# Rotary partners by four SP transfers from one whole ScalarE copy, in a two-layer attention kernel on one core

## What is computed

```python
def rope(x, pos):
    dh = x.shape[-1]
    freqs = ROPE_THETA ** (-jnp.arange(0, dh, 2, dtype=jnp.float32) / dh)
    ang = pos.astype(jnp.float32)[:, None] * freqs[None, :]
    cos = jnp.cos(ang)[None, :, None, :].astype(x.dtype)
    sin = jnp.sin(ang)[None, :, None, :].astype(x.dtype)
    x1, x2 = x[..., : dh // 2], x[..., dh // 2:]
    return jnp.concatenate([x1 * cos - x2 * sin, x2 * cos + x1 * sin], axis=-1)
...
q = rope(qkv[:, :, 0], pos)
k = rope(qkv[:, :, 1], pos)
```

## Time and profile before

| | us |
|---|---|
| median of three runs | 2187.29 |
| lowest and highest | 2184.91, 2189.29 |
| the profiled execution's own time | 2186.33 |
| its span, from first to last instruction | 2184.5 |
| busy: TensorE | 2103.2 (96%) |
| busy: VectorE | 955.9 (44%) |
| busy: ScalarE | 866.1 (40%) |
| busy: GpSimd | 837.4 (38%) |

### The profile page before, as it was taken

How to read it: one execution, slowest core, us unless ns; L and a number is a source line. 1 busy time by engine, 2 the same in 40 slices (tenths; PEclk the granted TensorE clock), 3 DMA queues, 4 the chain that set the end, 5 groups by cost and what they waited for, 6 DMA issues and landing times. The chain is left out here.

```text
span 2184.5 us, 26673 instructions
## 1 busy us (share of the span) xinstructions
PE 2103.2 (96%) x10336; PEld 1680.2 (77%) x10336; DVE 955.9 (44%) x1642; ACT 866.1 (40%) x1769; POOL 837.4 (38%) x447
## 2 busy tenths in 40 slices
PE   8999999999989989999999999999999899999998
PEld 6788898887768767778778788787774478888886
DVE  2454635544454585653442511268667532111212
ACT  4654556555364565542321332333332232221221
POOL 4423233333342332354444444334243152444443
PEclk9999999999999999999999999999999999999999
DMA  6322233223541312132443333332344242323331
GB/s 222 97 59 89 67 97 98 78 82 94 197 164 43 95 49 68 58 116 92 121 135 97 97 79 112 86 92 87 111 145 135 89 143 68 97 97 97 97 97 58
DMA packets 130204, 218.67 MB, mean 100 GB/s; under 512 B 8712, under 2 KB 58552, under 8 KB 129872
## 3 DMA queue, kind: packets, MB, share of 16 engines
q1 hardware_dynamic: 111152, 169.68, 26.0%
q0 software_dynamic: 8096, 28.93, 4.0%
q10 hardware_dynamic: 10832, 18.35, 2.4%
HBM read 198.29 MB, written 18.04 MB: 99 GB/s over the span
## 5 line engine op out<-in xcount | busy, mean ns | idle before, releaser
L2536 POOL TENSOR_TENSOR lo_ring<-raw_ring,hi_ring 128x1024 fp32r<-128x1024 f32 (+1 forms) x288 | 692.1, 2425 | 1002.2 <-ACT hi_ring L2179 1002.0
L1123 PE MATMUL bank<-xh,hi_ring 128*128 128x512 f32 (+1 forms) x1568 | 610.9, 390 | 3.5 <-DVE xl L1607 2.9
L1123 PE MATMUL bank<-xh,lo_ring 128*128 128x512 f32 (+1 forms) x1568 | 594.1, 379 | 0.0
L1123 PE MATMUL bank<-xl,hi_ring 128*128 128x512 f32 (+1 forms) x1568 | 592.8, 378 | 0.0
L2179 ACT CAST hi_ring<-raw_ring 128x1024 fp32r<-128x1024 f32 (+1 forms) x288 | 288.3, 1045 | 422.9 <-PE bank L1123 400.0
L1123 PEld LDWEIGHTS bank<-xh,hi_ring 128*128 128x128 f32 x1568 | 297.1, 190 | 66.3 <-issue 13.8
L1123 PEld LDWEIGHTS bank<-xh,lo_ring 128*128 128x128 f32 x1568 | 296.6, 189 | 56.2
L1123 PEld LDWEIGHTS bank<-xl,hi_ring 128*128 128x128 f32 x1568 | 297.4, 190 | 52.4 <-issue 1.9
L1123 PE MATMUL bank<-hi_ring,xh 128*128 128x512 f32 (+1 forms) x512 | 209.6, 409 | 8.2 <-DVE xl L1761 2.9
L1123 PE MATMUL bank<-hi_ring,xl 128*128 128x512 f32 (+1 forms) x512 | 201.4, 393 | 0.0
L1123 PE MATMUL bank<-lo_ring,xh 128*128 128x512 f32 (+1 forms) x512 | 201.3, 393 | 0.0
(11 more groups left out here) (289 smaller groups left out, 2650.1 us busy)
## 6 DMA issues: line engine op xcount, KB each, us to landing
raw_ring<-in_ffn_w_in SPq DMA_DIRECT2D x176, 256.0 KB, 3.2
raw_ring<-in_dil_w_in SPq DMA_DIRECT2D x80, 512.0 KB, 3.7
raw_ring<-in_ffn_w_out SPq DMA_DIRECT2D x44, 512.0 KB, 4.0
raw_ring<-in_diff_w_in SPq DMA_DIRECT2D x32, 512.0 KB, 3.8
raw_ring<-in_w_in SPq DMA_DIRECT2D x32, 512.0 KB, 3.7
arena<-scratch_heads POOLq DMA_DIRECT2D x4, 1584.0 KB, 13.8
scratch_gates<-arena ACTq DMA_DIRECT2D x24, 256.0 KB, 2.0
arena<-scratch_gates POOLq DMA_DIRECT2D x24, 256.0 KB, 5.2
```

Source lines behind the costliest of these rows:

```text
L1123: ins = T.matmul(bank[pb][:, cols if p.form == "feature" else slice(0, p.cols)], lhsT, rhs, start=(k == 0 and m == 0 and half != 1), stop= ...
L2536: G.tensor_tensor(lo, raw_ring[:, p % RAW, 0:q.kq * q.n], hi.bitcast(F32), ALU.subtract).then_inc(lowered, 1)
```

## The change

- ScalarE copies the whole bank once, 128 x 512, into `rope_b`. It waits first until `rope_rest` of the bank two before is done, since that reads the same half of `rope_b`.
- SP shifts: for each rotary bank four transfers of 32 partitions x 512 (64 KB), from `rope_b` to the partner's place in `QT` or `KT`, where the result will later stand. They signal `shifted`, one semaphore for even and one for odd banks.
- `rope_rest` waits for `shifted` in place of `drained`, takes the partner from `QT` or `KT` and writes the sin product into `rope_b`. It comes two banks later, not one, so that the cos products need a third place, the last 512 columns of `arena`.
- `rope_end` finishes the last two banks. It stands at the head of attention (directly before the first `d_score` or `f_score`) for units 0 to 3, 6 and 7, and behind the second `mac` of the `vt` panel for units 4 and 5.
- SP's program walks through the jobs. It loads up to 4 pieces beyond those that ScalarE splits at that job; in a rotary step it does so at bank 3, and in a panel's last step that is behind the shifts of banks 0 to 2. A shift waits for `drained`.
- Pool's load of the row `post0`, which lies in the third place, waits for all 48 banks of the dilated layer.

```diff
@@ rope_end: at the end of keys and projections before, now in attention
-        plan.job("rope_end")
...
+            if m == 1:
+                plan.job("rope_end", u)
...
         g = u // 2
+        if g < 2:
+            plan.job("rope_end", u)
@@ SP
+            def shift(p, o):
+                m = 4 * p.n + o
+                SP.wait_ge(drained[o], p.use[o])
+                for quad in range(4):
+                    SP.dma_start(rope_to(p, o)[32 * quad:32 * quad + 32], rope_b[32 * (quad ^ 1):32 * (quad ^ 1) + 32, m % 2, :]).then_inc(shifted[m % 2], 16)
...
+                elif kind == "mac":
+                    st = steps[a[0]]
+                    p = panels[st.panel]
+                    if place(*a) == st.look_at:
+                        wanted = st.ahead + RAW
+                    if p.kind != "rope" or a[1] == 3:
+                        load(wanted)
+                    if p.kind == "rope" and st.last and a[2:] != (0,):
+                        shift(p, a[1])
@@ VectorE
-            def rope_rest(which, u, o, m):
-                dst, b = (QT if which == "q" else KT)[:, u % 2, o, :], m % 2
-                V.wait_ge(drained[o], pending_use[m])
-                V.tensor_tensor(rope_b[:, b, :], rope_b[:, b, :], const("sin"), ALU.mult).then_inc(v_step, own.up())
+            def rope_rest(p, o):
+                m, dst = 4 * p.n + o, rope_to(p, o)
+                V.wait_ge(shifted[m % 2], 64 * (m // 2 + 1))
+                V.tensor_tensor(rope_b[:, m % 2, :], dst, const("sin"), ALU.mult).then_inc(v_step, own.up())
...
-                    if m >= 2:
-                        V.wait_ge(roped, m - 1)
-                    V.tensor_tensor(rope_a[:, o % 2, :], psum, const("cos"), ALU.mult).then_inc(cosed, 1)
-                    while pending:
-                        rope_rest(*pending.pop())
-                    pending.append((which, u, o, m))
+                    if m >= 3:
+                        V.wait_ge(roped, m - 2)
+                    V.tensor_tensor(cos_part[m % 3], psum, const("cos"), ALU.mult).then_inc(cosed, 1)
+                    if len(pending) == 2:
+                        rope_rest(*pending.pop(0))
+                    pending.append((p, o))
@@ ScalarE
                     A.wait_ge(cosed, m + 1)
-                    for quad in range(4):
-                        ins = A.copy(rope_b[32 * quad:32 * quad + 32, o % 2, :], psum[32 * (quad ^ 1):32 * (quad ^ 1) + 32, :])
-                    ins.then_inc(drained[o], 1)
+                    if m >= 2:
+                        A.wait_ge(roped, m - 1)
+                    A.copy(rope_b[:, m % 2, :], psum).then_inc(drained[o], 1)
```

More of the change, by code:

```diff
@@ L513, in keys @@
     def keys(u):
-        yield from plan.panel("rope", w, D + u * 512, 512, "feature", at=("k", 6 + u))
-        plan.job("rope_end")
+        return plan.panel("rope", w, D + u * 512, 512, "feature", at=("k", 6 + u))
     def attention(u):
@@ L521, in attention @@
         yield
+        plan.job("rope_end", 6 + u)
         for n in range(N + 4):
@@ L1004, in program @@
         y_panel = {p.w: p for p in panels if p.kind == "y" and p.at[0] == 1}
-        roped, cosed = sem("roped"), sem("cosed")
+        roped, cosed, shifted = sem("roped"), sem("cosed"), [sem(f"shifted{i}") for i in range(2)]
+        cos_part = [rope_a[:, 0, :], rope_a[:, 1, :], arena[:, ARENA - S:ARENA]]
         gate_tanhed, e_tanhed, hidden_rounded, hidden_made = sem("gate_tanhed"), sem("e_tanhed"), sem("hidden_rounded"), sem("hidden_made")
@@ L1057, in ready_value, with rope_to, load @@
             return made[name_value[0]], name_value[1]
+        def rope_to(p, o):
+            return (QT if p.at[0] == "q" else KT)[:, p.at[1] % 2, o, :]
         def sync_program(SP):
[L1060 to L1063, removed]
+            seen = Tally()
+            def load(limit):
+                while seen.n < min(limit, len(pieces)):
+                    p = seen.n
+                    seen.up()
+                    q = pieces[p]
+                    if p >= RAW:
+                        old = pieces[p - RAW]
+                        if old.parted:
+                            SP.wait_ge(lowered, old.split + 1)
+                        else:
+                            SP.wait_ge(*ready_value(steps[old.step].end))
+                    dst = raw_ring[:, p % RAW, 0:q.kq * q.n].rearrange("p (k n) -> p k n", k=q.kq)
+                    w = q.n // q.halves
+                    for i in range(q.halves):
+                        c = q.c0 + i * FFN
+                        src = I[q.w][q.k0 * P:(q.k0 + q.kq) * P, c:c + w].rearrange("(k p) n -> p k n", p=P)
+                        SP.dma_start(dst[:, :, i * w:(i + 1) * w], src).then_inc(landed[p % RAW], 16)
+            def shift(p, o):
[3 more added lines that the diff above has]
+                    SP.dma_start(rope_to(p, o)[32 * quad:32 * quad + 32], rope_b[32 * (quad ^ 1):32 * (quad ^ 1) + 32, m % 2, :]).then_inc(shifted[m % 2], 16)
+            wanted = RAW
+            for job in jobs:
+                kind, a = job.kind, job.at
+                if kind == "begin":
+                    SP.dma_start(consts[:, 0:P], I["consts"][:, 0:P]).then_inc(ident_landed, 16)
+                    SP.dma_start(x[:, 1, :], I["x"][P:2 * P, :]).then_inc(x_landed[1], 16)
+                    load(1)
@@ L1064, in sync_program @@
                     SP.dma_start(x[:, 3, :], I["x"][3 * P:4 * P, :]).then_inc(x_landed[3], 16)
-                if p == RAW:
+                    load(RAW)
                     SP.dma_start(consts[:, P:], I["consts"][:, P:]).then_inc(consts_landed, 16)
                     SP.dma_start(params[:, :], I["params"]).then_inc(consts_landed, 16)
[L1068 to L1079, removed]
+                elif kind == "lower_to":
+                    wanted = a[0] + RAW
+                    load(wanted)
+                elif kind == "mem_kv":
+                    wanted = steps[a[0]].ahead + RAW
+                    load(wanted)
+                elif kind == "mac":
[4 more added lines that the diff above has]
+                    if p.kind != "rope" or a[1] == 3:
+                        load(wanted)
+                    if p.kind == "rope" and st.last and a[2:] != (0,):
+                        shift(p, a[1])
@@ L1081, in tensor_program @@
+            load(len(pieces))
         def tensor_program(T):
@@ L1513, in vector_program @@
             pending = []
[L1515 to L1520 removed]
+            def rope_rest(p, o):
+                m, dst = 4 * p.n + o, rope_to(p, o)
+                V.wait_ge(shifted[m % 2], 64 * (m // 2 + 1))
+                V.tensor_tensor(rope_b[:, m % 2, :], dst, const("sin"), ALU.mult).then_inc(v_step, own.up())
+                r = DIL[p.at[1] // 2] if p.at[1] < 6 else 1
+                o_, a, c = dst, cos_part[m % 3], rope_b[:, m % 2, :]
                 if r > 1:
@@ L1526, in rope_rest @@
                 V.tensor_tensor(o_, a, c, ALU.add).then_inc(roped, 1)
-            pending_use = {}
             def consume(p, o):
@@ L1537, in consume @@
                 elif p.kind == "rope":
-                    which, u = p.at
                     V.wait_ge(filled[o], p.use[o])
-                    if which == "q" and u == 5 and o < 2:
-                        V.wait_ge(filled[6], use_of["v_turn", 2 + o][0])
-                    pending_use[m] = p.use[o]
-                    if m >= 2:
-                        V.wait_ge(roped, m - 1)
-                    V.tensor_tensor(rope_a[:, o % 2, :], psum, const("cos"), ALU.mult).then_inc(cosed, 1)
-                    while pending:
-                        rope_rest(*pending.pop())
-                    pending.append((which, u, o, m))
+                    if p.at == ("q", 5) and o == 0:
+                        V.wait_ge(filled[6], use_of["v_turn", 3][0])
+                    if m >= 3:
[4 more added lines that the diff above has]
+                    pending.append((p, o))
                 elif p.kind == "hid" and o < 2:
@@ L2029, in vector_program @@
                 elif kind == "rope_end":
-                    rope_rest(*pending.pop())
+                    while pending and pending[0][0].at == ("k", a[0]):
+                        rope_rest(*pending.pop(0))
                 elif kind == "norm_scale":
@@ L2582, in gpsimd_program @@
                 elif kind == "row":
+                    if a[0] == "post0":
+                        G.wait_ge(roped, 48)
                     if a[0] == "post1":
```

## The result

The changed kernel takes 2231.69 us, the median of four runs (2226.38 to 2233.66). Its ratio to the kernel before is 1.021, with a 95% interval of 1.020 to 1.023: slower by 2.1%, some 46 us over the 2186.1 us of the kernel before beside it, against the 13 us of the forecast. The profiled execution took 2233.66 us, its span 2231.9.

The account below looks back on a forecast made before the run. PE, busy 96% of the span, was taken to bound the kernel. Stalls of 14.4 plus clock loss of 7.1 less a gain of 8.2 gave +13.3 us on 2186.3: 2199.6 us, 0.6% slower, range 2191 to 2207.

Parts of the forecast that it names:

- the sin or add before them drawn out to the end of a Pool subtraction: Sign that the forecast is right: VectorE's sin or add before PE's `d_score` waits at units 0 to 3 lasts that long.
- part 2: SP and the transfers: copy end to `shifted` 3.1 us, bounds 1.1 and 7.3; loads still land in time, cost 0.
- any landing between 1.2 and 5 us gives the same: Last bank before attention: a landing that far behind the copy leaves the 14.4 us of stalls unchanged.
- rival (c): Last bank's transfers queue behind two loads, or copies held for `roped` delay exps: +8 to +12 us, 2208 to 2212; chance 0.11.
- part 3: Last bank before attention: longer chain stalls PE at `d_score` of units 0 to 3 by 4.9, 2.3, 3.1, 4.1: 14.4 us.
- "cost 0" at `f_score`: Units 4 and 5: chain of 9 us fits before `f_score`, five `mac` jobs behind the last bank, so no stall.
- The cover of 13.5 us: Five `mac` jobs between the last bank and `f_score` at units 4 and 5; if gone, some 3 us each.
- Pool's lock: Pool's subtractions block VectorE's last sin and add before `d_score`: stalls of 14.4 us, against 4.8 without the lock.
- Part 1, the gain: ScalarE's relief shortens PE's gaps near 774 and 817 us: 3.5 us plus 4.7 of clock, 8.2 us; least 3.5.
- 7.1 us for three gaps: Lower clock behind `d_score` gaps of units 0, 2 and 3, at 2.35 us each; between 0 and 4 x 3.1 = 12.4.

Follow-up runs that it names:

- Moving the loads: Changed kernel, but SP issues a rotary bank's four transfers first and the two 512 KB loads behind them: 2221.4 us, ratio 1.018.
- short subtractions: Changed kernel, but Pool subtracts only 8 of 1024 columns in pieces 8 to 135: 2204.9 us, ratio 1.009.
- one transfer: Changed kernel, but a bank's partner comes by one transfer of 128 partitions in place, halves not exchanged: 2202.9 us, ratio 1.009.
- one copy alone: Kernel before, but ScalarE copies the bank once, 128 partitions, partners not exchanged, no transfers: 2183.3 us, ratio 1.001.
- all three away: Changed kernel with one transfer per bank, loads behind the transfers, and Pool subtracting only 8 columns in pieces 8 to 135: 2177.7 us, ratio 0.998.

## Why the prediction was wrong

**Right: the place and the kind.** PE's waits at the first `d_score` of units 0 to 3, the clock at 0.50 behind them, ScalarE 113 us less busy, no `mac` late for weights (1.5 us at lo_ring against 2.2). The sign was right. The size was 46 us for 13, beyond the range. The mechanism that the forecast put at those waits is not the one found there: the sign "the sin or add before them drawn out to the end of a Pool subtraction" holds for the bank before the last only. The last sin and add took 0.69 us each, the add 1.04 where it is strided, at all four units.

**The step that failed: part 2, the time from copy to landing.** It was put at 3 x 0.37 + 2.0 = 3.1 us. From the copy's end to the sin product it was 7.3, 8.8, 8.9 and 11.3 us at units 0 to 3. With it fell the next step, that any landing between 1.2 and 5 us gives the same. Three parts were off.
- The issue. 0.368 us is the row of a load; a transfer of 64 KB inside SBUF takes SP 0.59 us, so a bank 2.4 us. The forecast took one kind's issue for another's.
- The queue and the engines. The loads directly ahead were priced as rival (c) at 1 to 2 us a unit. At unit 1 the four issues took 3.5 us and the last landed 4.7 us after they were over; at unit 3 (copy end 386.84, sin 398.15) one of the two loads ahead took 2.45 us to issue. Moving the loads took 9.8 us off the four waits and left 6.2 to 6.9 us from copy to use. The forecast also took no account of Pool's store of 1056 KB, which filled more than half of the DMA's time while unit 1's transfers were due. At unit 0, with two loads ahead but no store, the four issues took 2.4 us; at unit 1 3.5, and 3.8 with no load ahead. That the store did this is the reading that fits; it isn't shown by a run without it.
- The loop. The forecast held the last cos product of each unit where it was. But copy m waits for the add of bank m - 2, which waits for the transfers. The loop is copy, issues and landing, sin and add, and two banks share it. At unit 0 with the short subtractions, so without Pool, it reads 0.59 + 4.6 + 1.4 = 6.6 us, 3.3 for each bank, where PE fills one every 2.7: the copies come at 80.54, 83.80 and 87.20. With one transfer and the loads behind as well, they come 2.7 us apart (82.58, 85.30). In the changed kernel the last copy came at 89.39, where the old ones began at 85.8. The loads don't do this (moved, unit 0 kept 8.8 of 9.4 us); the number of issues does (one issue, 6.1), and Pool's drawn-out sin and add (short subtractions, 5.6).

With the issue short, the sum of part 3 is off by 2.6 us only (17.0 for 14.4), at units 2 and 3 by luck: late landing stands there in the place of Pool's subtractions.

**Part 3, "cost 0" at `f_score` and for the running unit.** The cover of 13.5 us was named, and its price if gone, 3 us. It was gone: VectorE had to pass two pairs of subtractions on the way, four of its operations took 2.15 to 2.85 us each (773.61 to 784.80). At `d_turn` VectorE's copy stood behind a transfer and a locked add (461.68 to 465.73); this is near to rival (c)'s second half, which has ScalarE's copies held for `roped`, as at 868.59. Rival (c) was the nearest of the rivals, with 0.11, and both its halves came. The first, at 4 to 8 us, was worth the 9.8 of the moved loads. The second, at 6 us, shows as gaps of 2 x 2.6 and 2.8 us. Its own time, 2208 to 2212, was still some 20 us short.

**Pool's lock.** The adds beside Pool's subtractions took 2.7 to 3.2 us in the changed kernel too, and the run with one transfer shows the chain that the forecast built on this. The Trainium skill, SBUF — State Buffer, section "Who interferes with whom", has a VectorE instruction with two SBUF inputs contend with a GpSimd instruction that reads SBUF; these rows agree. But in the changed kernel, where the transfers come after Pool's pair, it is no longer the last thing at units 1 to 3. Its 22 us lie mostly elsewhere: at unit 0, `f_score`, `d_turn` and the clock behind them.

**Part 1, the gain.** 8.2 us was forecast, 0 measured. Both gaps shrank by 2 us as forecast, and with one copy alone 3.1 us of the clock came back. It was taken again by new gaps: `d_score` waits of 4.1 us with the clock's 3.3 behind them, and 2.31 and 1.48 us near the two. What becomes late next was not asked of the freed engine's own followers.

**The clock.** 7.1 us for three gaps; measured 12.6 in the dilated layer with six. The price of a gap was about right, 2.1 us against 2.35; that there would be more and longer gaps was not foreseen. Six gaps of 36 us in sum cost 12.6, so 0.35 us for each us, where the forecast's three (12.1 us) had 0.6.

## What to carry to other kernels

- Before work goes from an engine's copies to transfers, add up the loop in which the scratch returns: copy, all issues in series, landing, use. If it is longer than buffers times period, every bank is late, not only the last.
- Several small transfers cost one issue each on their queue, and what the program puts directly ahead of them counts in full. Look for the bulk load that stands there, and for bulk stores of other queues that share the DMA engines.
- Relieving one engine brings its later work forward too. Ask whom that will meet.

## What the runs showed of the hardware

- The issue of a 64 KB transfer within SBUF held SP for a median of 0.59 us, a 256 KB one 0.47 us, a 512 KB load 0.37 in the kernel before. Beside a 1056 KB store of Pool, four took 3.5 us behind loads and 3.8 with no load ahead, and one load's issue took 2.45 us (387.37).
- A 256 KB transfer within SBUF landed in 2.3 us (median), and in 5.2 where the same store had 62% of the DMA engines' time and nothing stood ahead of it on its own queue (all three away, unit 2). The store itself landed in 4.7 us in the kernel before and in 9.0 in the changed one.
- An add with both inputs in SBUF that began 0.47 us before Pool's first subtraction still lasted until 0.9 us behind the second, 6.08 us (unit 2, one copy). The same add of the kernel before, with a lead of 0.40 us, took 1.15. In the slow case Pool was issuing a store when the add began, in the fast one Pool was idle. The Trainium skill, SBUF — State Buffer, section "Who interferes with whom", says that issue order decides who blocks. The fast row agrees (Pool's first subtraction took 2.87 us there, against 2.40); in the slow one the add began before the subtractions and was drawn out all the same, and whether the store's issue is the reason no run shows.
- The granted clock fell behind gaps of PE of 2.57 and 2.58 us too (0.51 from 466 to 468 us, 0.55 from 558 to 560), not only at those of 5.7 to 9.4.
